# The MLP's down projection by seven products of halves in place of eight

## What is computed

```python
u = _rmsnorm(h, mlp_norm_g[l])
h = h + jnp.square(jax.nn.relu(u @ w_up[l])) @ w_down[l]
...
h = _rmsnorm(h, final_norm_g)
return h[:, N_META:]
```

## Time and profile before

| | before |
|---|---|
| median of 3 runs | 1016.01 us (1015.92 to 1016.11) |
| the profiled execution's own time | 1016.66 us |
| its span, first to last instruction | 1014.9 us |
| granted TensorE clock over it | 0.999 of full speed |
| busy: PE, DVE, ACT, POOL | 99%, 51%, 41%, 58% of the span |

### The profile page before, as it was taken

One profiled execution on the slowest core, in us unless ns is written; L12 is line 12 of the kernel. 1 busy time (PEld: TensorE's weight loads), 2 busy tenths in 40 slices (PEclk: granted clock), 3 DMA queues, 4 the chain that ended last, 5 costly groups with the idle time before them and its releaser, 6 DMA issues.

```text
span 1014.9 us, 12887 instructions
## 1 busy us (share of the span) xinstructions
PE 1004.7 (99%) x4967; PEld 849.0 (84%) x4967; DVE 522.1 (51%) x879; ACT 420.1 (41%) x689; POOL 583.9 (58%) x724
## 2 busy tenths in 40 slices
PE   9999999999999999999999999999999999999997
PEld 7888788888888888888899977888888888888886
DVE  5781256665374743445679988865123213312324
ACT  4553355555562224443246685554222222222332
POOL 4555455664756874564658878456545545545470
PEclk9999999999999999999999999999999999999999
DMA  7323222112453125323223122322322342243132
GB/s 231 115 83 100 83 84 82 44 42 84 125 169 111 56 80 189 126 83 102 64 84 109 59 84 87 95 79 94 124 87 79 104 132 76 83 130 99 63 104 83
DMA packets 84829, 99.16 MB, mean 98 GB/s; under 512 B 3698, under 2 KB 69904, under 8 KB 84768
## 3 DMA queue, kind: packets, MB, share of 16 engines
q1 hardware_dynamic: 84464, 98.07, 30.1%
q10 hardware_dynamic: 304, 0.27, 0.1%
HBM read 96.23 MB, written 2.10 MB: 97 GB/s over the span
## 4 chain that ended last, share of the span: by engine, by line
PE 92%; DVE 5%; ACT 1%; issue 1%; DVEq 0%; ACTq 0%
PE ps L455 62%; PE ps L474 19%; PE ps L865 2%; PE ps L600 1%; PE ps L524 1%; PE ps L621 1%; PE ps L585 1%; PE ps L584 1%; PE ps L662 1%; PE ps L507 0%; DVE Hl L1399 0%; DVE tmp L1896 0%; PE ps L500 0%; DVE Al L2050 0%; PE ps L691 0%
## 5 line engine op out<-in xcount | busy, mean ns | idle before, releaser
L2159 POOL TENSOR_TENSOR wlo<-raw,whi 128x256 fp32r<-128x256 f32 x648 | 505.3, 812 | 326.0 <-ACT whi L873 325.9
L873 ACT ACTIVATE whi<-raw 128x1024 fp32r<-128x1024 f32 (+1 forms) x164 | 172.2, 1050 | 148.5 <-PE ps L474 91.0
L455 PE MATMUL ps<-Hh,whi 128*128 128x512 f32 x512 | 201.9, 394 | 0.7 <-DVE Hl L1399 0.7
L455 PE MATMUL ps<-Hl,whi 128*128 128x512 f32 x512 | 199.5, 390 | 0.0
L455 PE MATMUL ps<-Ah,whi 128*128 128x512 f32 (+1 forms) x576 | 196.5, 364 | 0.2 <-DVE Al L2050 0.2
L455 PE MATMUL ps<-Al,whi 128*128 128x512 f32 (+1 forms) x576 | 194.8, 361 | 0.0
L455 PE MATMUL ps<-Hh,wlo 128*128 128x512 f32 x512 | 129.3, 389 | 0.3 <-POOL wlo L2159 0.3
L455 PE MATMUL ps<-Ah,wlo 128*128 128x512 f32 (+1 forms) x576 | 124.4, 360 | 0.0
L455 PEld LDWEIGHTS ps<-Ah,whi 128*128 128x128 f32 x576 | 103.0, 188 | 16.9 <-DVE Al L2050 0.8
L455 PEld LDWEIGHTS ps<-Al,whi 128*128 128x128 f32 x576 | 103.0, 188 | 15.9
L455 PEld LDWEIGHTS ps<-Hh,whi 128*128 128x128 f32 x512 | 96.2, 188 | 20.8 <-DVE Hl L1399 1.4
(11 more groups left out here) (309 smaller groups left out, 1187.7 us busy)
## 6 DMA issues: line engine op xcount, KB each, us to landing
raw<-in_w_in SPq DMA_DIRECT2D x29, 1024.0 KB, 5.4
raw<-in_w_up SPq DMA_DIRECT2D x16, 1024.0 KB, 5.3
raw<-in_w_down SPq DMA_DIRECT2D x32, 512.0 KB, 3.3
raw<-in_w_in SPq DMA_DIRECT2D x14, 512.0 KB, 3.7
raw<-in_w_att_out SPq DMA_DIRECT2D x4, 1024.0 KB, 5.1
raw<-in_w_sg_out SPq DMA_DIRECT2D x4, 1024.0 KB, 5.1
raw<-in_w_o SPq DMA_DIRECT2D x4, 1024.0 KB, 5.0
Fm<-in_x SPq DMA_DIRECT2D x1, 2048.0 KB, 7.8
```

The lines of the kernel that those rows point to most:

```text
L455: mm = e.matmul(ps[:, bk, 0:c1 - c0], of(j)[:, k % kk, 128 * g:128 * g + 128], x[:, k, c0:c1], start=(start and n == 0), stop=(stop and n ...
L873: return e.activation(out, src, ACT.Copy, scale=scale)
L2159: ins = e.tensor_tensor(w_lo(j)[:, *cut], raw_tile(j)[:, *cut], f(w_hi(j))[:, *cut], ALU.subtract)
```

## The change

The down projection of a part is a product of X (512 rows x 1024 features) and W (1024 features x 1024 columns). The change cuts rows, features and columns in half: X into four blocks of 256 x 512, W into four quarters of 512 x 512. Instead of eight products of halves it makes seven (`P11`, `P_7`, `P_5`, `P12`, `P_6`, `P_3`, `P_4`, in this order), four of them on a sum of quarters of W (`w_sum`) and four on a difference of blocks of X (`x_sums`). Each product has two weight tiles of 256 features (h = 0, 1) and 12 matmuls for each: eight on the high weights, then four on the low. Of the fourteen tiles of a part POOL makes eleven low parts and DVE three (`LOW_BY_DVE`, `w_low`). The weights of the down projection no longer go through the raw buffers: each quarter (1 MB) is loaded whole (`load_quarter`), and the sums stand in the place of quarter (0, 1) or in spare buffers. The activations stay in `X`, unsplit, and their high and low parts are made for each product (`a_high` on ACT and `a_low` on DVE, 128x1024 each), in three slots.

The results of `P11`, `P_7`, `P_5` and `P_6` are gathered over the parts in `acc`, in F4 (`out`); those of `P12`, `P_3` and `P_4` go straight into `OT`. In the last part `spread_sums` adds what is gathered from the three parts ahead into the four quarters of the output, eight chained instructions of 128x1024, and `last_out` puts each product of the last part where it belongs. All eight `residual` turns stand in the up projection of part 0 (five before).

```diff
-        for h in range(2):
-            for k in range(4):
-                cols("w_down_2", 1024 * i + 256 * k, 512 * h, 1, 2, 1)
+        tiles.extend((None, (i, n, h)) for n in range(7) for h in range(2))
...
+P11, P_7, P_5, P12, P_6, P_3, P_4 = range(7)
+LOW_BY_DVE = ((P_7, 1), (P12, 1), (P_3, 1))
...
+        X = sb("X", [128, 8, 512])
+        w12_w22 = sb("w12_w22", [128, 3072])
+        x_part = sb("x_part", [128, 2048], R32)
+        x_sum_7 = sb("x_sum_7", [128, 1024])
...
+        quarters = {(0, 0): F2f[:, 0:2048], (1, 0): F2f[:, 2048:4096], (0, 1): w12_w22[:, 0:2048],
+                    (1, 1): tmpf[:, 0:2048]}
+        w_sum3 = [by2(P[:, 1024:2048]), by2(w12_w22[:, 2048:3072])]
+        acc = [by2(F4f[:, 1024 * i:1024 * i + 1024]) for i in range(4)]
+        acc_of = {P11: 0, P_7: 1, P_5: 2, P_6: 3}
...
+                else:
+                    w.wait_ge("w_sum5", (part - 1, 1))
+                    w.wait_ge(*low_ready(down_tile(part - 1, P11, 1)))
+                    load_quarter(part, 0, 0)
+                    w.wait_ge(*low_ready(down_tile(part - 1, P12, 0)))
+                    w.wait_ge(*low_ready(down_tile(part - 1, P12, 1)))
+                    w.wait_ge("w_sum4", (part - 1, 1))
+                    load_quarter(part, 1, 0)
+                    w.wait_ge(*low_ready(down_tile(part - 1, P_3, 0)))
+                    w.wait_ge(*low_ready(down_tile(part - 1, P_3, 1)))
+                    load_quarter(part, 1, 1)
+                    w.wait_ge(*low_ready(down_tile(part - 1, P_4, 1)))
+                    load_quarter(part, 0, 1)
...
+            def down(part, n):
+                xh, xl = x_slot(part, n)
+                w.wait_ge("a_high", (part, n))
+                for h in range(2):
+                    j = down_tile(part, n, h)
+                    w.wait_ge("hi", j)
+                    ks = (2 * h, 2 * h + 1)
+                    for low in range(2):
+                        for r in range(2):
+                            if h == 0 and low == 0:
+                                w.wait_ge(*down_free(part, n, r))
+                            for k, x in ([(k, xh) for k in ks] if low else [(k, x) for x in (xh, xl) for k in ks]):
+                                if x is xl:
+                                    w.wait_ge("a_low", (part, n))
+                                if low:
+                                    w.wait_ge(*low_ready(j))
+                                of = w_lo if low else w_hi
+                                mm = e.matmul(ps[:, down_bank(n, r), :], x[:, k, 128 * r:128 * r + 128], of(j)[:, k % 2],
+                                              start=(h == 0 and low == 0 and k == 0 and x is xh), stop=(h == 1 and low == 1 and k == 3))
+                            if low and (h or r):
+                                mm.then_inc(*b.done("products", (j, r)))
+            def down_free(part, n, r):
+                if n >= 4:
+                    return "down_out", (part, n - 4, r)
+                if part == 0 and n == 3:
+                    return "residual_set", 7
+                return "drained", up_tile(part, (2, 4, 6, 0)[n] + r)
...
+            xh, xl = x_slot(3, P_4)
+            w.wait_ge("a_low", (3, P_4))
+            order = [(k, w_hi, x) for k in range(4) for x in (xh, xl)] + [(k, w_lo, xh) for k in range(4)]
+            for r, c0, c1, bk in ((0, 0, 512, 4), (1, 0, 256, 5), (1, 256, 512, 6)):
...
+                for i in range(14):
+                    if part < 3 or i < 12:
+                        cast(down_tile(part, 0, i) + 2)
+                    for n in {1: (P_5,), 2: (P12,), 4: (P_6,), 8: (P_3,), 9: (P_4,)}.get(i, ()):
+                        a_high(part, n)
...
+            def x_sums(part, n):
+                one, other, old = {P_7: (x_half(1, 0), x_half(0, 0), None), P_5: (x_half(1, 0), x_half(1, 1), None),
+                                   P_6: (x_half(0, 0), x_sum, P_5), P_3: (x_half(0, 1), x_sum, P_6)}[n]
+                w.wait_ge("act_set", (part, 3 if n == P_7 else 7))
+                if old is not None:
+                    w.wait_ge("a_low", (part, old))
+                elif part:
+                    w.wait_ge("a_low", (part - 1, P_3))
+                e.tensor_tensor(x_operand(n), one, other, ALU.subtract).then_inc(*b.done("x_sum", (part, n)))
...
+            def w_sum(part, n, h):
+                out = w_sum3[h] if n == P_7 else quarter(0, 1, h)
+                if n == P_7:
+                    w.wait_ge("quarter01_in", part)
+                    w.wait_ge("quarter11_in", part)
+                    if part:
+                        w.wait_ge(*low_ready(down_tile(part - 1, P_7, h)))
+                elif n == P_5:
+                    w.wait_ge("w_sum7", (part, h))
+                    w.wait_ge("quarter00_in", part)
+                else:
+                    w.wait_ge("quarter10_in", part)
+                    w.wait_ge(*low_ready(down_tile(part, P_5 if n == P_6 else P_6, h)))
+                other = {P_7: (1, 1), P_5: (0, 0), P_6: (1, 1), P_4: (1, 0)}[n]
+                name = {P_7: "w_sum7", P_5: "w_sum5", P_6: "w_sum6", P_4: "w_sum4"}[n]
+                e.tensor_tensor(out, quarter(0, 1, h), quarter(*other, h), ALU.add).then_inc(*b.done(name, (part, h)))
...
+            def last_out(n):
+                for r in range(2):
+                    bank = ps[:, down_bank(n, r), :]
+                    w.wait_ge("products", (down_tile(3, n, 1), r))
+                    signal = b.done("down_out", (3, n, r))
+                    if n == P_6:
+                        w.wait_ge("down_out", (3, P11, r))
+                        e.tensor_tensor(acc[3][:, r], bank, acc[0][:, r], ALU.subtract).then_inc(*signal)
+                        continue
+                    if n in (P11, P12):
+                        y, y2 = y_half(0, 0)[:, r], None
+                    else:
+                        y, y2 = y_half(1, 1)[:, r], y_half(1, 0)[:, r] if n == P_7 else y_half(0, 1)[:, r]
+                    w.wait_ge("vector_step")
+                    e.tensor_tensor(y, y, bank, ALU.add).then_inc(*(signal if n == P12 else step()))
+                    if n == P11:
+                        e.tensor_copy(acc[0][:, r], bank).then_inc(*signal)
+                    elif n != P12:
+                        e.tensor_tensor(y2, y2, bank, ALU.subtract if n == P_7 else ALU.add).then_inc(*signal)
+            def spread_sums():
+                add(acc[3], acc[0], ALU.subtract)
+                add(y_half(0, 0), acc[0])
+                add(acc[2], acc[3])
+                add(y_half(0, 1), acc[2])
+                add(y_half(1, 1), acc[2])
+                add(y_half(1, 1), acc[1])
+                add(y_half(1, 0), acc[1], ALU.subtract)
+                add(y_half(1, 0), acc[3], ALU.subtract)
+            for part in range(4):
+                last = part == 3
                 if part:
...
+                    out(part - 1, P_4)
+                for n in range(4):
                     act(part, n)
...
+                x_sums(part, P_7)
+                act(part, 4)
+                a_low(part, P11)
+                w_sum(part, P_7, 0)
+                act(part, 5)
+                a_low(part, P_7)
+                w_sum(part, P_7, 1)
+                act(part, 6)
+                if last:
+                    spread_sums()
+                w_sum(part, P_5, 0)
+                w_sum(part, P_5, 1)
+                act(part, 7)
+                x_sums(part, P_5)
+                a_low(part, P_5)
+                w_low(part, P_7, 1)
+                last_out(P11) if last else out(part, P11)
+                a_low(part, P12)
+                x_sums(part, P_6)
+                last_out(P_7) if last else out(part, P_7)
+                w_sum(part, P_6, 0)
+                w_sum(part, P_6, 1)
+                a_low(part, P_6)
+                w_low(part, P12, 1)
+                last_out(P_5) if last else out(part, P_5)
+                x_sums(part, P_3)
+                last_out(P12) if last else out(part, P12)
+                a_low(part, P_3)
+                w_sum(part, P_4, 0)
+                w_low(part, P_3, 1)
+                if not last:
+                    out(part, P_6)
+                    w_sum(part, P_4, 1)
+                    a_low(part, P_4)
+                    out(part, P_3)
+            w_sum(3, P_4, 1)
+            last_out(P_6)
+            a_low(3, P_4)
...
+            w.wait_ge("down_out", (3, P_6, 1))
+            add(y_half(0, 1), acc[3])
+            w.wait_ge("final_g_in", 0)
+            for r in range(2):
+                times_g(r, 0, 512, "first_times", r)
+            e.tensor_tensor(y_half(1, 1), y_half(1, 1), acc[3], ALU.add).then_inc(*b.done("y22_set", 0))
+            add(y_half(1, 0), acc[3], ALU.subtract)
+            w.wait_ge("y22_set", 0)
+            for r in range(2, 4):
+                times_g(r, 512, 512, "first_times", r)
+            for r in range(2):
+                last_add(r, 0, down_bank(P_3, r), 512, 512)
```

(66 more changed lines are left out.)

299 lines of the change are left out of this document (162 added, 137 removed).

## The result

The changed kernel takes 1040.34 us (median of 4 runs, 1040.05 to 1040.76) against 1016.06 for the kernel before on the same chip: ratio 1.0239, 95% interval 1.0221 to 1.0257. It is slower by 24.3 us; 1038.0 with a range of 1020 to 1047 was predicted. The profiled execution took 1040.76 us, its span is 1038.9.

The account below looks back on a forecast made before the run. TensorE alone was taken to set the MLP's time before the change; 1016.66 + 1.5 (part 0) - 0.2 (middle parts) + 21 (part 3) = 1039, less 0.65 for profiled execution over median: 1038 us, range 1020 to 1047.

Parts of the forecast that it names:

- What goes: Down projections: 24 fewer matmuls a part at 0.2267 us, 5.44 us each, four times 21.8 us; a part lasts 38.1.
- The price of meeting: POOL against DVE in SBUF: DVE's 1024 columns take +0.42 us, POOL gets one instruction per 1.65 instead of 0.71.
- 0.84: First block: what each DVE instruction takes from POOL, (9.00 - 5.66) / 4 us, with four of DVE's inside eight instructions.
- The middle parts, 43.4: Down projections of parts 1 and 2: each ends at 43.4 us against 43.52 before, -0.1 each.
- T10: 1.6 late: Middle parts, weight tile T10: POOL's low part ready at 34.35 us, due at 32.7.
- Part 0, +1.5: Part 0's down projection: late act(7) on DVE, up to 2 us more late, +1.5 us.
- Part 3, +21: Part 3's down projection to the end: `spread_sums` and `last_out` make DVE the bound, +21 us (undisturbed +14).
- DVE without a gap: Part 3: DVE at work without a gap from act(6) to the end, as a sign of the forecast.
- Mild meeting: Rival, chance 0.15: POOL loses half of what the rows show; part 3 +17, a part saves some 3.4: 1023 us.
- faster: Rival, chance 0.10: POOL and DVE do not hold each other up in the MLP, low parts in time: 1013.7 us.
- full block: Rival, chance 0.07: each DVE instruction takes its whole 1.22 us from POOL, + 2.3 in each of four parts: 1047.
- The clock's fall: Rival, chance 0.06: the clock falls to 0.50 behind TensorE's wait at T3 in part 3, up to +3 us: 1041.

Follow-up runs that it names:

- nine_dve: The kernel of `three` with T9's low part moved to DVE too, behind out for `P_5`: 1013.72 us, ratio 0.9974.
- before_dummy: The kernel before, with fifteen unused 128x1024 additions on DVE after the last act of parts 0 to 2: 1017.58 us, ratio 1.0013.
- pool_one: The changed kernel with POOL's low part of each down tile in one 128x1024 instruction instead of four of 128x256: 1046.8 us, ratio 1.03.
- warm: The changed kernel with twelve unused matmuls on TensorE ahead of T6's low part in parts 0 to 2: 1038.88 us, ratio 1.0222.
- high_first: The changed kernel with part 0's high parts for `P11` and `P_7` ahead of the two residual copies on ACT: 1035.81 us, ratio 1.0193.
- spread_up: The changed kernel with the eight `spread_sums` additions two by two behind act(3, 0) to act(3, 3): 1030.35 us, ratio 1.0138.
- three: The changed kernel with the edits of `spread_up`, `high_first` and `t5_dve` together: 1024.66 us, ratio 1.0073.
- t5_dve: The changed kernel with T5's low part on DVE instead of POOL, and T7's low part ahead of that for `P_6`: 1037.0 us, ratio 1.0205.

## Why the prediction was right, and where it was not

- **What goes.** Right: the matmuls cost nothing but their own time, and where TensorE waits for only 0.8 us a part's down projection takes 39.75 us, 1.65 over the 38.1 of the sum (`nine_dve`).
- **The price of meeting.** Right: 1.65 and 1.65 were taken, 1.62 and 1.66 measured (`before_dummy`). The page "SBUF — State Buffer" of the Trainium skill, section "SBUF: two separate sides", has the loser blocked for the whole instruction. By that rule a turn of one of each is 0.71 + 1.22 = 1.93 us; the run disagrees for short instructions, by 0.27 a turn. Which part of POOL's instruction runs beside DVE's, as the prediction has it, no run shows. With POOL's instruction four times as long the picture is nearer to the rule: POOL's ends at 811.58, and 1.22 behind that would be 812.80; DVE's ends at 812.66 (`pool_one`). One reading of the rows was loose: of the "four of DVE's" that gave 0.84, the one at 350.16 has a single tensor for input; nothing was worked out from the 0.84.
- **The middle parts, 43.4.** The sum was right, 43.5 and 43.6. T5 was 0.4 late and T6 2.7, where 0.7 and 3.05 were given. "T10: 1.6 late" does not show in the changed kernel, and the step that dismissed the clock there ("the 3.05 us in the middle parts are shorter than the 4 us after which it fell") was wrong: the clock did fall. The two stand for each other: half clock used up what TensorE would have waited at T10, and with the clock held up T10 is 1.1 late (`warm`).
- **Part 0, +1.5.** Too small by 3.4: it was 4.9, 3.6 in the down projection and 1.3 for the turns moved ahead of it. The two copies ahead of each high part were named, but their cost was put at 2.6 us; DVE's waits on ACT were 5.8 and 1.6 us, act(7) ended 6.2 us into the down projection (709.50 by the timeline), and T3 was late by 1.9. Without them part 0 is 5.0 shorter (`high_first`). That the whole still came within 2.3 us of 1038 is in part luck: this execution reached the MLP 1.0 us early, and part 3 came out 0.9 under its term.
- **Part 3, +21.** Right in sum: +20.1. TensorE waited 7.0 us at T3, where 5 to 8 were given. Of "DVE without a gap" 49.97 of 51.4 us hold. DVE had the low part for `P_4` done at t = 45, not 48, and took 24 us from there to the end, not 22. Wrong was that TensorE's last matmul would end some 17 us ahead of the end: it ended 6.8 us ahead (1031.26 + 0.87 against 1038.9). The sum let the last product wait for DVE alone and run 5.4 us. It began 2.5 us later than given (1020.07, t = 50.5), because `P_3` ahead of it had waited 2.7 us for POOL, stood 3.5 us for POOL's last low part, which meets DVE's additions, and ran most of the rest at half clock (0.50 from 1027 to 1030): 12.1 us for the product. The end was DVE's in any case, so this cost nothing that the chain shows. Of the +21, 10 are now known to be the place of the additions (`spread_up`).
- **The rivals.** Mild meeting and faster are out by `before_dummy`; full block by the same run. The clock's fall happened in every part, and was nearly free in the middle ones; in part 3 its share was not measured.

What stays open: why the clock fell behind some waits and not behind others of the same length, where the runs of `three` that were not profiled lost their time, and how much of part 3's remaining 8.9 us is DVE's own work. 51.87 of its 58.1 us are DVE busy, so most of it should be, but that is argued and not tried.

## What to carry to other kernels

Before you trade TensorE's work for additions, count what the additions take from the other engine that reads SBUF, not only what they take themselves: here one of DVE's 128x1024 cost 0.4 us on DVE and 0.95 on POOL. Neither a delay nor longer instructions helped in this kernel; moving a tile to the engine that does it in one instruction did, since it takes 2.83 us from POOL and costs some 1.7 on DVE. Look first at order: eight additions in the wrong place were 10.0 of the 24.3 us lost, and two copies ahead of each of two casts 4.5.

## What the runs showed of the hardware that was not expected

- The granted clock. In the changed kernel a wait of 2.69 us at T6 was followed by over 3 us at 0.50; in part 1 of `t5_dve` a wait of 2.66 us at T9 was followed by 1.00 throughout. The place is not what tells them apart, for in the profile of `three` the same wait at T9, behind the same work, was followed by 1.00 in parts 0 and 2 and by 0.50 in part 1. TensorE's rows of parts 0 and 1, four matmuls in 1.21 and in 2.08 us:

```profile
732.77 1.21 PE L923 MATMUL ps<-wlo,Hl 128*128 128x512 f32 x4 [2.66 <-POOL wlo L2429]
817.74 2.08 PE L923 MATMUL ps<-wlo,x_part 128*128 128x512 f32 x4 [2.67 <-POOL wlo L2429]
```

- POOL does 128x1024 in one instruction in 2.40 us undisturbed, and in four of 128x256 in 2.83. From the timeline of `pool_one`:

```profile
823.91 2.40 POOL L2429 TENSOR_TENSOR wlo<-tmp,whi 128x1024 fp32r<-128x1024 f32 x1 [1.14 <-ACT whi L975]
```
